# A conditioned decoder layer on one core: modulation units, start loads, casts and start products put in another order

## What is computed

```
c_act = jax.nn.silu(c)
mod = (c_act @ w_ada[l] + b_ada[l]).reshape(B, N_SUB, N_MOD, D_MODEL)

h = modulate(rms_norm(x, norm_ffn1_g[l]), mod[:, 0, 0], mod[:, 0, 1])
x = x + HALF_STEP * mod[:, 0, 2][:, None, :] * swiglu(h, ffn1_w_in[l], ffn1_w_out[l])

h = modulate(rms_norm(x, norm_mix_g[l]), mod[:, 1, 0], mod[:, 1, 1])
proj = h @ w_mix_in[l]
...
x = x + mod[:, 1, 2][:, None, :] * mix

h = modulate(rms_norm(x, norm_ffn2_g[l]), mod[:, 2, 0], mod[:, 2, 1])
x = x + HALF_STEP * mod[:, 2, 2][:, None, :] * swiglu(h, ffn2_w_in[l], ffn2_w_out[l])
return rms_norm(x, norm_final_g)
```

## Time and profile before

| | us |
|---|---|
| median of 3 runs | 888.24 (887.46 to 888.37) |
| the profiled execution | 887.46 |
| its span, first to last instruction | 885.7 |
| PE busy | 858.6 |
| DVE busy | 584.3 |
| ACT busy | 331.7 |

### The profile page before, as it was taken

The page is one execution under the profiler, slowest core; times in us unless marked ns, Lnnn a source line. Parts: engine busy times, 40 slices in busy tenths (PEclk is TensorE's granted clock), DMA queues, the critical chain, the costliest instruction groups (busy, mean ns, idle before and its releaser), DMA issues.

```text
span 885.7 us, 13665 instructions
## 1 busy us (share of the span) xinstructions
PE 858.6 (97%) x5290; PEld 744.6 (84%) x5290; DVE 584.3 (66%) x902; ACT 331.7 (37%) x434; POOL 36.0 (4%) x42
## 2 busy tenths in 40 slices
PE   4899999999999999999999999999999999999997
PEld 3678888888888888897887898899988899999886
DVE  4579777777777756538645469988633588885443
ACT  6232222222223221225424356666521256655223
POOL 0000000000000000000340000000000000100000
PEclk9899999999999999999999999999999999999998
DMA  9978666666667555434533322576343476663322
GB/s 273 287 199 244 189 190 191 190 190 191 192 179 207 168 164 174 146 104 110 144 95 95 94 74 72 135 178 171 83 131 94 117 185 159 151 155 91 98 66 95
DMA packets 219483, 134.44 MB, mean 152 GB/s; under 512 B 5560, under 2 KB 214572, under 8 KB 219436
## 3 DMA queue, kind: packets, MB, share of 16 engines
q1 hardware_dynamic: 216500, 128.52, 50.8%
q0 software_dynamic: 2880, 5.24, 3.6%
q10 hardware_dynamic: 56, 0.01, 0.0%
HBM read 126.41 MB, written 2.10 MB: 145 GB/s over the span
## 4 chain that ended last, share of the span: by engine, by line
PE 90%; DVE 6%; ACT 2%; SPq 1%; DMA 1%; issue 1%; ACTq 0%
PE ps L1558 22%; PE ps L1560 21%; PE ps L1559 21%; PE ps L1935 7%; PE ps L1931 7%; PE ps L1933 7%; DVE h_lo L1010 1%; PE ps L1813 1%; PE ps L1814 1%; PE ps L1815 1%; DMA w_raw<-in_ffn_w_in_dram 1%; PE ps L1749 1%; DVE sw_lo_a L1436 1%; DVE w_split L968 1%; DVE xs L1003 0%
## 5 line engine op out<-in xcount | busy, mean ns | idle before, releaser
L1558 PE MATMUL ps<-h_hi,w_split 128*128 128x512 f32 (+1 forms) x464 | 182.4, 393 | 8.8 <-DVE h_lo L1010 8.6
L1560 PE MATMUL ps<-h_hi,w_split 128*128 128x512 f32 (+1 forms) x464 | 179.2, 386 | 0.0
L1559 PE MATMUL ps<-h_lo,w_split 128*128 128x512 f32 (+1 forms) x464 | 178.0, 384 | 0.0
L957 DVE TENSOR_TENSOR w_split<-w_raw,w_split 128x2048 fp32r<-128x2048 f32 (+1 forms) x45 | 93.3, 2073 | 76.6 <-ACT w_split L601 76.6
L1558 PEld LDWEIGHTS ps<-h_hi,w_split 128*128 128x128 f32 x464 | 87.9, 189 | 27.9 <-issue 6.0
L601 ACT CAST w_split<-w_raw 128x2048 fp32r<-128x2048 f32 (+1 forms) x45 | 77.1, 1712 | 81.2 <-PE ps L1560 72.8
L1560 PEld LDWEIGHTS ps<-h_hi,w_split 128*128 128x128 f32 x464 | 87.7, 189 | 19.1
L1559 PEld LDWEIGHTS ps<-h_lo,w_split 128*128 128x128 f32 x464 | 87.8, 189 | 17.5
L1054 DVE SCALAR_TENSOR_TENSOR ada_acc<-ada_raw,c_act,ada_acc 128x256 f32<-128x256 f32 x196 | 95.0, 485 | 7.0
L1931 PE MATMUL ps<-sums_hi,sw_hi 128*128 128x256 f32 x320 | 89.6, 280 | 0.9 <-DVE sw_lo_a L1436 0.5
L1933 PE MATMUL ps<-sums_lo,sw_hi 128*128 128x256 f32 x320 | 89.8, 281 | 0.0
(11 more groups left out here) (186 smaller groups left out, 1532.6 us busy)
## 6 DMA issues: line engine op xcount, KB each, us to landing
ada_raw<-in_w_ada_dram SPq DMA_DIRECT2D x56, 512.0 KB, 3.7
sw_raw<-in_ffn_w_in_dram SPq DMA_DIRECT2D x100, 256.0 KB, 4.1
w_raw<-in_ffn_w_in_dram SPq DMA_DIRECT2D x48, 512.0 KB, 6.1
ada_first<-in_w_ada_dram SPq DMA_DIRECT2D x16, 512.0 KB, 7.4
w_raw<-in_ffn_w_out_dram SPq DMA_DIRECT2D x16, 384.0 KB, 4.0
w_raw<-in_w_mix_in_dram SPq DMA_DIRECT2D x12, 512.0 KB, 4.4
sw_raw<-in_ffn_w_out_dram SPq DMA_DIRECT2D x16, 384.0 KB, 4.1
w_raw<-in_ffn_w_out_dram SPq DMA_DIRECT2D x16, 320.0 KB, 3.3
```

The source lines that it names most:

```text
L957: nc.vector.tensor_tensor(w_lo[s][:, 0:n], w_raw[s][:, 0:n], w_hi[s][:, 0:n].bitcast(F32), ALU.subtract).then_inc(lo_ready, 1)
L1558: nc.tensor.matmul(dst, w_h, a_h, start=start, stop=False)
L1559: nc.tensor.matmul(dst, w_h, a_l, start=False, stop=False)
L1560: return nc.tensor.matmul(dst, w_l, a_h, start=False, stop=stop)
```

## The change

It has six parts, and none changes what is computed or how many instructions do it.

1. The loads of `c`, `b_ada` and `g1` move from SP's queue to ACT's, ahead of the four there.
2. `first_rows_of(7)` on PE moves behind `first_products(5, 1)`, where it stood ahead of it.
3. On DVE, U(j) stands ahead of S(j) and not behind it, for all j but 0. SP's loads of the units move one place ahead to go with it.
4. In the down part SP's loads are put in a plain pattern: two halves of a block, then one unit.
5. `sum_units(0, 22)` on PE stands right behind the first half of the first down block, and not within the second half.
6. On ACT, ahead of the first `strassen`, `cast_up(0, 1)` stands behind `hsum_split(1)` and `hsum_split(2)`, and `cast_up(0, 2)` moves behind `keep_sum(0, 0)`.

```
@@ SP
-            load_vec("c", c)
-            load_vec("b_ada", b_ada)
-            load_vec("g1", norm_ffn1_g)
             for t in range(NT):
                 load_x(t)
...
                 load_pair(ffn1_w_in, j + 2, j, UP1 + j + 2)
                 load_ada(j)
+            load_ada(2)
             with sp.Fori(1, KF // 2 - 1) as i:
                 for s in range(2):
                     load_pair(ffn1_w_in, i * 2 + (s + 2), s, i * 2 + (s + 2 + UP1))
-                    load_ada(i * 2 + s)
-
-            for s in range(2):
-                load_down(ffn1_w_out, 0, s, DOWN1 + s)
-                load_ada(KF - 2 + s)
-            for s in range(2):
-                load_down(ffn1_w_out, 1, s, DOWN1 + 2 + s)
-            load_ada(KF)
-            with sp.Fori(1, (UNITS - KF) // 2) as i:
+                    load_ada(i * 2 + (s + 1))
+            load_ada(KF - 1)
+
+            with sp.Fori(0, (UNITS - KF) // 2) as i:
                 for q in range(2):
                     for s in range(2):
                         load_down(ffn1_w_out, i * 2 + q, s, i * 4 + 2 * q + s + DOWN1)
-                    load_ada(i * 2 + q + (KF - 1))
+                    load_ada(i * 2 + q + KF)
             for m in range(UNITS - KF, KD):
                 for s in range(2):
                     load_down(ffn1_w_out, m, s, DOWN1 + 2 * m + s)
-                if m == UNITS - KF:
-                    load_ada(UNITS - 1)
@@ ACT
+            load_vec("c", c)
+            load_vec("b_ada", b_ada)
+            load_vec("g1", norm_ffn1_g)
             load_vec("gmix", norm_mix_g)
...
             plain_silu(0)
             hsum_split(0)
-            for c in range(3):
-                cast_up(0, c)
+            cast_up(0, 0)
             hsum_split(1)
             hsum_split(2)
+            cast_up(0, 1)
             plain_hi(0)
             plain_silu(1)
...
+                if n == 0:
+                    cast_up(0, 2)
                 keep_five(n)
@@ DVE
                 first = isinstance(jn, int) and jn == 0
+                if ada and not first:
+                    ada_unit(j)
+
                 dve.wait_ge(silu_ready, jn + 1)
...
-                if ada:
+                if ada and first:
                     ada_unit(j)
@@ PE
                         for k in range(KC):
-                            if not last and s == 1 and k == KC // 3 and isinstance(m, int) and m == 0:
-
-                                sum_units(0, KF)
...
                         ins.then_inc(chunk_done, 1)
+                        if not last and s == 0 and isinstance(m, int) and m == 0:
+
+                            sum_units(0, KF)
...
             for k in range(3, KD - 1):
                 first_rows_of(k)
-                first_products(k - 1, 0)
-                if k == KD - 2:
-                    first_rows_of(KD - 1)
-                first_products(k - 1, 1)
+                for s in range(2):
+                    first_products(k - 1, s)
+            first_rows_of(KD - 1)
```

4 lines of the change are left out of this document (removed).

## The result

| | before | changed |
|---|---|---|
| median of 4 runs, us | 888.31 (887.46 to 889.33) | 900.39 (899.85 to 901.71) |
| profiled execution, us | 887.46 | 900.13 |
| its span, us | 885.7 | 898.4 |
| PE busy, us | 858.6 | 861.3 |

The changed kernel takes 1.0138 times as long (95% interval 1.012 to 1.0155), 12.1 us in the medians and 12.7 us between the two profiled executions. The forecast was 896.0 us with a range of 892.5 to 899.0: the sign was right, but the result lies above the range by 1.4 us, and 4.4 us above the forecast. PE has the same work as before, so most of the 12.7 us is time in which PE stands still or runs at the lower clock. Now and then an execution of most kernels here, the one before too, came out 3 to 6 us longer than the rest, so a median is given with its interval and read beside the trace.

What follows compares the result with a forecast made beforehand. PE was taken as the bound, with losses only where it stands still. Part 1 0.1 + part 2 1.1 + part 3 4.0 + part 6 2.6 = +7.8 us, forecast 896.0 us against 888.24, range 892.5 to 899.0.

Steps and rivals of the forecast that it cites:

- What bounds the kernel: PE busy 858.6 of 885.7 us, and 220.00 of 220.00 from 80 to 300 us; gains possible only where PE stands still.
- the landing of the last vector: Start, on ACT's queue: issued at about 3.1 us, landing 2.76 us later at 5.8, so part 1 costs +0.1 us.
- the clock behind the new gap: PE after its wait at step 3: the sum counted 4.0 us for the gap and no term for a slower clock.
- The bound: Part 1 at the start: gain ends at -0.92 us, loss has no such end; +1.0 us if landing takes 3.7 us.
- (a): Rival, chance 0.15: PE's clock falls at the new 4.0 us gap at step 3, costing 1.7 us; time 897.7.
- (b): Rival, chance 0.10: PE's clock stays at 2.4 GHz at the start, twelve matmuls save 2.4 us; 893.6.
- (c): Rival, chance 0.02: start gains up to 3.3 us and U(1) hides wholly; 888.2 or a tenth or two under the old.
- (d): Rival, chance 0.07: U(1)'s load at step 3 lands in 7.0 us, not 3.7; part 3 costs 7.3 us; 899.3.

## Why the prediction was wrong, and where it was right

**What bounds the kernel** held. From 80 to 300 us PE is busy for 220.00 us again; only the clock's mean is 0.99 there, for the tail of the slow stretch behind step 3. But for that tail, nothing is lost in the stretch that was said to be full. Two terms of the sum were wrong, though: the landing of the last vector, and the clock behind the new gap, which the sum had at nothing.

**Part 1 is the step that failed.** Its issue times were right (3.16 for a forecast 3.1, `x` at 0.80). The term of the landing was not: 2.76 us was taken from the row of "this very transfer", and it measured 5.34. That row had been taken in other traffic, with `x` started only 0.1 us before it, and in the changed kernel `x` starts with the first of the seven, 2.4 us before the last. The bound failed too: the loss was said to have no end, and yet the most that was priced was +1.0 us, by a landing of 3.7 us, the middle value of a row whose slowest landing was 7.0. With 5.34 the rest of the step's own arithmetic is right. The vectors come 8.50 - 4.85 = 3.65 us later, ACT's row ends at 19.92 in place of 16.27 (3.65 again), and its cast starts 3.65 - 0.92 = 2.7 us later, as it no longer waits for the weights; it measured 19.82 - 17.19 = 2.6, and the first product 23.03 - 20.41 = 2.6. The forecast's term was 0.1. At step 2 the 4.6 us are these 2.6, the 1.1 of part 2 and the 0.9 of a larger clock loss in the start; whether part 1 makes that last one isn't shown.

The Trainium skill, page "DMA: Bandwidth & Descriptors", section "Issuing engines are not separate DMA queues", says that transfers started by different engines run on the same 16 DMA engines and interleave. As far as it goes the trace agrees: the last tile of `x`, issued at 2.2 us, landed 6.7 us later, at 8.9, just after the vectors at 8.5. What I drew from it, that small loads are not held behind large ones, does not stand there, and the runs refute it: 1.48 us alone, 5.34 us beside `x`.

**Part 2** was right in its wait: 1.5 us forecast, 1.48 in the changed kernel and 1.49 alone. Its time alone came out 1.8 us longer in the medians, for +1.1.

**Part 3** was right in every link of its gap: a wait of 4.13 us for 4.0; a unit behind two waits for its load of 0.64 and 0.46 us, in place of one of 0.8 and a short one; weight block 4 late, its cast released by the load at 81.91, and no further wait of PE behind it. That cast was forecast at 77.1 and came 4.8 us later, with step 3 itself 4.9 us later than forecast (78.22 for 73.3), so that it still had its cover ahead of PE. The 4.9 is the start's: 4.61 us of it stands at step 2 already.

**Parts 4 and 5** cost nothing, as no wait in the trace bears their names. **Part 6** was right: DVE idle for 2.49 us for a forecast 2.6, and PE's waits in and at the end of the first `strassen` 1.80 + 2.07 = 3.9 us for "some 4.2".

**The rivals.** (a), the clock falls at the new gap, is what happened, at 0.15; it was priced at 1.7 us and measured 1.7. The row for it was there: one gap of 4.60 us followed by 0.53, against none of that length without a fall. To leave the clock out of the sum, at a chance of 0.15 against the only example, is the second step that failed. The Trainium skill, page "TensorE: Matmul & The Clock Gate", section "Why this matters for your kernels", warns that a gap in PE's work can drop it to the lower clock. The runs agree: the gaps of 3.81, 3.92, 4.13 and 4.43 us at a step were each followed by a lower clock, and the two that were filled were not. (b), the clock stays up at the start, did not come: the clock loss there is 4.1 us. It was also priced too low, since the twelve matmuls that it counts leave out the small matmuls of the same slow stretches: by the stretches shown above they cost 3.2 us in the kernel before, not 2.4. (c) and (d) did not come: U(1) waited 1.1 us in sum, about the 1.0 of the forecast.

The sum with the corrections, 2.5 for the vectors, 0.9 for the clock of the start and 1.7 for that behind step 3: 7.8 + 2.5 + 0.9 + 1.7 = 12.9 us, against 13.4 at the second checkpoint and 12.7 in the span.

**What stays open.** The medians of the four kernels with one part each are 2.7, 1.8, 9.2 and 2.6 us over that of the kernel before, 16.3 in sum, while the changed kernel is 12.1 over. At the second checkpoint the parts add up no better: 3.7 + 1.5 + 8.0 + 4.0 are 17.2 against 13.4. Of the difference, 2.2 us is step 2 itself, which came 1.0 and 1.2 us late in the two kernels whose start was not edited; of the other 1.6 us, about 0.3 is the longer gap of parts 3 to 5 alone (4.43 for 4.13) and 0.8 its longer slow stretch (2.5 for 1.7). So a part's own price is known to about 1 us and not better. Why some executions without a profile take 2 to 4 us more than the traced one is not shown: for parts 3 to 5 their mean clock is the same, while for the changed kernel without part 1 it is 0.988 to 0.989 where the traced execution has 0.993.

## What to carry to other kernels

The small loads on which the first chain waits go first on every queue, and the bulk right behind them: here, moving three of them to the other queue started the bulk 1.18 us sooner and the first product 2.6 us later. Take a landing time only from a row with the traffic that the changed kernel will have. Price a new wait of PE of 4 us as its length and a stretch at half the clock on top, 1.7 to 2.5 us here. If it can't be closed, fill it with idle matmuls that end before the data come: 14 that ended in time gave back 2.0 us, and the fills that ran over gave back less than they saved in clock. Where a loop's order is rotated, count what stands between the first two steps, as the steady state hides it.
